# Expert weight loads of a 32-slot mixture-of-experts stage: one transfer a chunk for gate and up, expert numbers read ahead of a wait, down-projection halves reloaded one by one

## The reference, cut to what matters

```python
for e in range(N_EXPERTS):
    he = jax.nn.silu(t @ w1[e]) * (t @ w3[e])
    y = y + gates[:, e:e + 1] * (he @ w2[e]).astype(jnp.float32)
```

## Time and profile before

| what | value |
|---|---|
| median of 3 runs | 1234.81 us |
| lowest and highest | 1231.45 and 1239.08 us |
| the profiled execution's own time | 1233.89 us |
| its span, first to last instruction | 1232.0 us |
| PE busy in the span | 1091.4 us (89%) |
| DVE, ACT, POOL busy | 707.4, 514.1, 354.1 us |
| mean granted TensorE clock | 0.947 |
| chain of waits, share | PE 60%, DMA 12%, DVE 7%, issue 7% |
| of it transfers into `below` from the expert weights | 7% |
| of it SP issuing at L1370 | 3% |

### The profile page before, as it was taken

How to read it: one execution, slowest core, us unless ns; L and a number is a source line. 1 busy time by engine, 2 the same in 40 slices (tenths; PEclk the granted TensorE clock), 3 DMA queues, 4 the chain that set the end, 5 groups by cost and what they waited for, 6 DMA issues and landing times.

```text
span 1232.0 us, 18370 instructions
## 1 busy us (share of the span) xinstructions
PE 1091.4 (89%) x5873; PEld 882.0 (72%) x5873; DVE 707.4 (57%) x1348; ACT 514.1 (42%) x935; POOL 354.1 (29%) x379
## 2 busy tenths in 40 slices
PE   5999999998888899999999999974899999999930
PEld 4889899965456777777878786863777777778820
DVE  4430610136656666566566655438777777777757
ACT  4433321122531221323223233313777878778803
POOL 3100510001531111011111100101665656566657
PEclk9999999999989898898999999986999999999975
DMA  8340141141769585555655454834988786867476
GB/s 279 100 159 1 52 139 50 44 111 48 252 230 345 182 294 193 190 205 179 213 190 202 157 173 143 297 132 154 315 311 315 242 291 232 289 233 265 189 236 253
DMA packets 105765, 242.84 MB, mean 197 GB/s; under 512 B 15248, under 2 KB 63840, under 8 KB 95456
## 3 DMA queue, kind: packets, MB, share of 16 engines
q0 software_dynamic: 23328, 122.17, 28.3%
q1 hardware_dynamic: 81312, 117.42, 27.9%
q10 hardware_dynamic: 1056, 2.36, 0.6%
HBM read 243.31 MB, written 48.94 MB: 237 GB/s over the span
## 4 chain that ended last, share of the span: by engine, by line
PE 60%; DMA 12%; DVE 7%; issue 7%; POOL 5%; ACT 5%; SPq 4%; POOLq 1%; ACTq 0%; DVEq 0%
DMA below<-in_w 7%; PE ps L1027 5%; PE ps L889 4%; PE ps L907 4%; PE ps L2130 4%; PE ps L2131 4%; PE ps L2132 4%; PE ps L985 3%; PE ps L1065 3%; SPq L1370 3%; PE ps L1066 3%; PE ps L2125 3%; PE ps L2124 3%; PE ps L2126 3%; PE ps L1069 3%
## 5 line engine op out<-in xcount | busy, mean ns | idle before, releaser
L1787 DVE TENSOR_TENSOR low<-below,high 128x1024 fp32r<-128x1024 f32 x128 | 156.7, 1257 | 38.0 <-ACT high L1484 36.1
L1582 PE MATMUL ps<-high 128*128 128x512 f32 x384 | 157.1, 409 | 13.9 <-DVE low L1797 7.4
L1456 POOL TENSOR_TENSOR low<-below,high 128x1024 fp32r<-128x1024 f32 x64 | 132.8, 2076 | 97.5 <-ACT high L1504 96.4
L1583 PE MATMUL ps<-low,high 128*128 128x512 f32 x384 | 151.7, 395 | 0.0
L1584 PE MATMUL ps<-high,low 128*128 128x512 f32 x384 | 151.6, 395 | 0.0
L1484 ACT ACTIVATE high<-below 128x1024 fp32r<-128x1024 f32 x128 | 130.5, 1068 | 42.8 <-DMA below<-in_w 42.5
L626 ACT ACTIVATE arena<-ps 128x512 f32<-128x512 f32 (+8 forms) x100 | 50.0, 510 | 178.1 <-PE ps L889 177.7
L889 PE MATMUL ps<-arena 128*128 128x128 f32 (+4 forms) x613 | 96.6, 281 | 10.1 <-ACT arena L869 3.8
L770 POOL DMA_DIRECT2D high<-wo_dram x34 | 18.6, 547 | 298.9 <-PE ps L1069 287.1
L1582 PEld LDWEIGHTS ps<-high 128*128 128x128 f32 x384 | 72.9, 190 | 30.9 <-issue 15.5
L889 PEld LDWEIGHTS ps<-arena 128*128 128x128 f32 (+4 forms) x613 | 73.7, 152 | 28.6 <-issue 17.3
(11 more groups left out here) (246 smaller groups left out, 2239.2 us busy)
## 6 DMA issues: line engine op xcount, KB each, us to landing
below<-in_w SPq DMA_DIRECT2D x256, 256.0 KB
high<-wo_dram POOLq DMA_DIRECT2D x36, 1024.0 KB, 5.3
low<-wo_dram POOLq DMA_DIRECT2D x36, 1024.0 KB, 8.0
below<-in_w POOLq DMA_DIRECT2D x64, 512.0 KB
y_dram<-arena SPq DMA_DIRECT2D x32, 512.0 KB
arena<-in_x_prompt SPq DMA_DIRECT2D x15, 512.0 KB
below<-in_w_in SPq DMA_DIRECT2D x14, 512.0 KB, 7.6
out<-arena SPq DMA_DIRECT2D x9, 512.0 KB, 2.6
```

The lines of the kernel that those rows point to most:

```text
L1456: pool.tensor_tensor(w2_lo[s % UN][:, c], w2_in[:, c], w2_hi[s % UN][:, c].bitcast(F32), ALU.subtract).then_inc(s_w2lo, 1)
L1582: pe.matmul(out, x_hi, w_hi, start=start, stop=False)
L1583: pe.matmul(out, x_hi, w_lo, start=False, stop=False)
L1787: dve.tensor_tensor(chunk(w13_lo[j], c), chunk(w13_in, c), chunk(w13_hi[j], c).bitcast(F32), ALU.subtract).then_inc(s_w13lo, 1)
```

## The change

Four things are changed. (1) The host joins `w1` and `w3` along the last axis into `w13`, and SP loads a chunk of both in one transfer of 512 KB with rows of 2 KB; the waits of ACT and DVE count 16 a slot where they counted 32. (2) SP's store of output rows moves from behind the four chunks of slot s (row s - 3) to ahead of the chunks of slot s and behind the reads of the expert numbers (row s - 4); four stores are left for the end instead of three. The order of transfers on SP stays the same, but for the nine residual loads of slot 28, which now come ahead of the store of slot 25 instead of behind it. (3) POOL reads the expert numbers of slot s + 1 ahead of its waits for the high parts. (4) POOL issues the load of each half of `w2` right behind the low part of that half.

```diff
             e, new = expert(sp, s)
-            rows13 = [w[0, bass.ds(e, 1)].rearrange("e (c p) f -> p (e c) f", p=P) for w in (w1, w3)]
+            rows13 = w13[0, bass.ds(e, 1)].rearrange("e (c p) f -> p (e c) f", p=P)
+            if not isinstance(s, int) or s >= 4:
+                store_y(s - 4)
+                sp.dma_start(y_dram[bass.ds((s - 4) * P, P), :], y_row[:, j, :]).then_inc(s_yst[j], 16)
             for c in range(WC):
...
                     sp.wait_ge(s_w13lo, split)
-                for k in range(2):
-                    sp.dma_start(w13_in[:, 2 * c:2 * c + 2, k * FF:(k + 1) * FF], rows13[k][:, 2 * c:2 * c + 2, :],
-                                 cond=new).then_inc(s_w13in[c], 16)
-            if not isinstance(s, int) or s >= 3:
-                store_y(s - 3)
-                sp.dma_start(y_dram[bass.ds((s - 3) * P, P), :], y_row[:, (j + 1) % UN, :]).then_inc(
-                    s_yst[(j + 1) % UN], 16)
+                sp.dma_start(w13_in[:, 2 * c:2 * c + 2, :], rows13[:, 2 * c:2 * c + 2, :],
+                             cond=new).then_inc(s_w13in[c], 16)
...
-        for s in range(SLOT_TILES - 3, SLOT_TILES):
+        for s in range(SLOT_TILES - 4, SLOT_TILES):
...
-        def load_second(s):
-            e, new = expert(pool, s)
-            for c in range(2):
-                if s:
-                    pool.wait_ge(s_w2lo, 2 * s + c - 1)
-                pool.dma_start(w2_in[:, c], w2[0, bass.ds(e, 1), c * P:(c + 1) * P].rearrange("e p n -> p (e n)"),
-                               cond=new).then_inc(s_w2in[c], 16)
+        def load_second(s, c, e, new):
+            if s:
+                pool.wait_ge(s_w2lo, 2 * s + c - 1)
+            pool.dma_start(w2_in[:, c], w2[0, bass.ds(e, 1), c * P:(c + 1) * P].rearrange("e p n -> p (e n)"),
+                           cond=new).then_inc(s_w2in[c], 16)
...
             if s + UN < SLOT_TILES:
                 gather(s + UN)
+            if s + 1 < SLOT_TILES:
+                e, new = expert(pool, s + 1)
             for c in range(2):
                 pool.wait_ge(s_w2hi, 2 * s + c + 1)
                 pool.tensor_tensor(w2_lo[s % UN][:, c], w2_in[:, c], w2_hi[s % UN][:, c].bitcast(F32),
                                    ALU.subtract).then_inc(s_w2lo, 1)
-            if s + 1 < SLOT_TILES:
-                load_second(s + 1)
+                if s + 1 < SLOT_TILES:
+                    load_second(s + 1, c, e, new)
...
-                act.wait_ge(s_w13in[c], 32 * (s + 1))
+                act.wait_ge(s_w13in[c], 16 * (s + 1))
...
-                dve.wait_ge(s_w13in[c], 32 * (s + 1))
+                dve.wait_ge(s_w13in[c], 16 * (s + 1))
...
+    inputs["w13"] = np.concatenate([inputs["w1"], inputs["w3"]], axis=-1)
```

More of the change, by code:

```diff
@@ L104, in hybrid_layer @@
                  kv_norm, w_uq, w_uk, w_uv, hg_lb_logits, hg_gnorm, w_o, ffn_norm, w_router_group, b_router_group,
-                 w_router_expert, b_router_expert, w1, w3, w2, final_norm, table, level_masks,
+                 w_router_expert, b_router_expert, w13, w2, final_norm, table, level_masks,
                  y_prompt, y_sample, ckv_prompt, krope_prompt, hgrn_prompt, ckv_sample, krope_sample, hgrn_sample):
@@ L1447, in moe_pool @@
         gather(0)
-        load_second(0)
+        e, new = expert(pool, 0)
+        for c in range(2):
+            load_second(0, c, e, new)
         gather(1)
@@ L2216 @@
         "kv_norm", "w_uq", "w_uk", "w_uv", "hg_lb_logits", "hg_gnorm", "w_o", "ffn_norm", "w_router_group",
-        "b_router_group", "w_router_expert", "b_router_expert", "w1", "w3", "w2", "final_norm"]
+        "b_router_group", "w_router_expert", "b_router_expert", "w13", "w2", "final_norm"]
 _OUTS = [(1, 1024, D), (1, SAMPLE, D), (1, 1, 1024 + META, CR), (1, 1, 1024 + META, RD), (1, 1, HH, HK, HK),
@@ L2229 @@
     arrays, args = {}, []
+    inputs["w13"] = np.concatenate([inputs["w1"], inputs["w3"]], axis=-1)
     for name, a in [(n, np.ascontiguousarray(inputs[n])) for n in _INS] + [("table", table), ("masks", level_masks)]:
-        if name in ("w1", "w2", "w3"):
+        if name in ("w13", "w2"):
             a = np.ascontiguousarray(a.reshape(1, NG, EG, *a.shape[2:]).swapaxes(1, 2).reshape(a.shape))
```

## The result

The changed kernel takes 1237.71 us (median of 12 runs, 1234.48 to 1243.71) against 1233.45 (12 runs) of the kernel before: ratio 1.0033, 95% interval 1.0018 to 1.0048. It is slightly slower, where 1.1% faster was forecast, and stands outside the forecast's range. The profiled execution took 1234.48 us with a span of 1232.8, 0.6 us more than that of the kernel before. It was the fastest of the 12, 3.2 us under their median, so the traces show only a part of the loss of 4.3 us between the medians.

A forecast was written before the change was run, and what follows sets the result against it. PE's pace of 9.36 us a slot was the floor, expert loads adding 20.8 us. Gains of 10.5 (slots 8 to 27) and 4.0 (slots 0 to 8), less 0.5, made 14.0 us: 1221 us, range 1217 to 1223.

The forecast's parts named there:

- Halves of w2: POOL's w2 loads: half 0 reloaded 0.1 us after its low part instead of 2.1; half 1's low part 0.6 later, costing nothing.
- Slower: Rival: half 0's issue delays POOL's low part of half 1, the down product waits for it in 31 slots; 1246, chance 0.03.
- Pairs: Slots 8 to 27, a new expert every second slot: earlier last chunk removes 10.5 of 11.4 us excess, ends 4 and 11.4.
- 3.15 MB at 354 GB/s: Down weights, tokens, gate and up ahead of the last chunk's landing from about 1004: 8.9 us, landing at 1013.6 against 1016.19.
- Followers: Slots 0 to 8, new experts in succession: 4.0 of 9.4 us excess gained, ends 1.0 and 9.4.
- The engines hold the landing: Rival: the last chunk lands when the bytes are through; slots 8 to 27 give 5, slots 0 to 8 2; 1228, chance 0.27.
- One transfer a chunk: SP's chunk loads: four issues at 0.5 us each let SP follow DVE; last chunk issued 2.1 to 2.5 us earlier.
- Reads ahead of the wait: SP's expert-number reads moved ahead of the store: first chunk issued 0.9 us sooner; alone cannot be worse than nothing.
- Slot 28: Nine residual loads go ahead of slot 25's store: cost 0 with 4 us cover, 3 us once if the cover is gone.
- Rows of 2 KB: Chunk loads run at 386 GB/s instead of 354, saving 0.5 us a new expert; bounds nothing and 0.75 us.

The follow-up runs named there:

- parts 1 and 2: Kernel before with SP's side of the change only (one transfer a chunk, store behind the expert reads), POOL's code as before: 1230.84 us, ratio 0.9983.
- joined weights alone: Kernel before with only w1 and w3 joined, one 512 KB transfer a chunk in 2 KB rows: 1230.77 us, ratio 0.9961; again 1227.51, 0.9967.
- cutting w2: Kernel with SP's side of the change only, loads of w2 cut to 64 of 1024 columns from slot 1 on: 1220.34 us, ratio 0.9876.
- the order alone: Kernel before with only SP's store of output rows moved behind the expert reads and ahead of the chunks: 1236.79 us, ratio 1.0023.
- changed kernel with the cut: Changed kernel with POOL's low part of half 1 cut to 64 of 1024 columns from slot 2 on: 1225.34 us, ratio 0.9928.
- parts 3 and 4: Kernel before with POOL's side only (expert reads ahead, each w2 half loaded behind its own low part), SP as before: 1247.81 us, ratio 1.0125.
- the delay alone: Kernel before with POOL waiting for its half 0 low part and reading expert numbers between its two low parts: 1252.59 us, ratio 1.0150.
- the store behind chunk 0: Joined weights and expert reads ahead, against the kernel before, with the output rows stored after the first chunk's load: 1255.91 us, ratio 1.0192.

## Why the prediction was wrong, step by step

The forecast was 14.0 us less, and the medians show 4.3 more. Some 10 of these 18 us are the overlap, which the forecast did not have. Without it the change is worth 0.9948, some 6.4 us; the other 7.6 of the 14.0 were expected of transfers that come through more slowly than forecast. Both are estimates from ratios.

**Halves of w2** is the step that gave the wrong sign. "Cover 3.5 us, cost nothing" looked for who waits for the low part of half 1, found the down product, and stopped. The cover held. The price came from what runs beside the instruction at its new time. In the kernel before, the second of POOL's low parts starts 2.2 us after the first (896.45 and 898.64), and DVE's four hardly meet it: they take 4.82 us, and 4.63 where that low part is cut. In the changed kernel it starts 3.5 us after (997.63 and 1001.14) and meets them, which costs DVE 1.36 us more in slot 15. The delay was mis-sized too: 0.6 us forecast, 1.3 measured, since POOL's wait for its own result was not in it. The two engines shut each other out: DVE's first low part ends at 1004.36 (1004.18 + 0.18 in the chain), its own length of 1.2 us behind POOL's end at 1003.17, and not behind its own start at 1001.48. By an estimate from these rows, their need is 2 x 2.0 + 4 x 1.2 = 8.8 us of exclusive time in a slot of 9.36, so there is hardly a place to move either to. Removing the overlap turns 1.0033 into 0.9948. The rival "Slower" named this very instruction and its delay, but let it decide through the down product, and set 0.03.

The Trainium skill, SBUF — State Buffer, section Who interferes with whom, states that a DVE instruction with two SBUF inputs contends with a GpSimd instruction that reads SBUF. Section SBUF: two separate sides of that page adds that whichever of the two starts first has the shared pair of ports for its whole length, and the other "fully blocks". The traces agree in both directions (6.18 for 4.82 us on DVE, 3.04 for 2.0 on POOL). Both low parts are such instructions, and the forecast did not weigh it.

**Pairs** was mis-sized: 10.5 us forecast, 2.9 measured with parts 1 and 2, and 1.1 without the half-clock stretch. (The forecast also counted on the load of half 0 in the idle gap, which is part 4's.) The issue came earlier as said. Counted from DVE's first low part, the last chunk is issued at 5.09 us (1000.97 to 1006.06) where it was 7.43 (1001.54 to 1008.97): 2.3 of the 2.1 to 2.5. The joined weights alone do as much (1000.77 to 1005.87, 5.10), so the order adds nothing there. But ACT takes it 13.68 us after that first low part (1014.65) where it was 14.65 (1016.19): 1.0 of the 2.6. The term that failed is 3.15 MB at 354 GB/s. That rate is of chunk rows alone on the engines; the first 5 us of these bytes move at 282. Were it so for all of them, 3.15 MB would take 11.2 us and not 8.9, 2.3 more, which is an upper bound; the landing came at 1014.63 (1006.06 + 8.57), 1.0 past the forecast's 1013.6, although that execution stood 0.6 us ahead of the other at 1001.

**Followers**: 4.0 forecast, none measured. The 2 KB rows do run at 390 GB/s (396 with parts 1 and 2, 1010 to 1014), but slots 0 to 8 wait for the sum of chunks, halves and tokens, and cutting w2 shows it: 6.2 us come back there. The rival "The engines hold the landing" (1228) was nearest to parts 1 and 2, which took 1230.84; it had followers at 2 and pairs at 5, and neither came.

**One transfer a chunk** was right: SP now follows DVE, four issues in 3.65 us, and the last goes out 0.3 us after its buffer is free (1007.66 to 1007.92 in the changed kernel). Joined weights bring 0.3 to 0.4% by themselves (0.1 to 0.6% by the intervals).

**Reads ahead of the wait** "cannot be worse than nothing" was false: the order alone costs 0.2% (1.0007 to 1.0038). Counted from DVE's first low part, the first chunk goes out at 1.81 us (1001.65 to 1003.46) where it was 2.30 (1001.54 to 1003.84), 0.5 of the 0.9 forecast. The step counted SP's time alone; that a chunk that goes out sooner takes the engines from a half of w2 fits the traces and is not shown. **Slot 28** was right: ACT at L1497 waited there only for PE, and keeping the residual loads in place brought nothing.

**Rows of 2 KB**: 386 forecast, 390 and 396 measured. The Trainium skill's limit of about 358 GB/s for a core between HBM and SBUF (DMA: Bandwidth & Descriptors, section Where 436 GB/s comes from), by which longer rows bring nothing, does not hold in these traces, in which one core is at work.

## What to carry to other kernels

Before an instruction is moved, even by 1 us, lay its new place beside what the other engines run then, and ask what they share; the cover to its own consumer is only half of the question. Reckon a landing with the rate that the same mixture of transfers shows in the trace, not with the best row of the same kind, and ask whose bytes an earlier issue pushes back. Run each part of a change by itself: here only the first of four parts gained beyond the noise as it stood, and together they lost. Parts 3 and 4 were never run one by one.

## What the runs showed of the hardware

- DVE and POOL, each with a two-input `tensor_tensor` on SBUF, exclude each other: the later one waits for the earlier one's end. The mean of 128 low parts went from 1257 to 1440, 1470 and 1476 ns in the three kernels that separate POOL's two low parts, and to 1236 where one of them was cut. A DVE operation with one input in PSUM is not held: the low part of the gated rows takes 0.42 us beside POOL's low part (parts 1 and 2, 1000.02) and away from it (changed kernel with the cut, 993.61).
- Rate by row length on an engine share above 1: 354 GB/s with 1 KB, 390 and 396 with 2 KB, 405 with 4 KB. Mixed with POOL's halves and the gather: 282 to 289 at a share of 0.9.
- TensorE's granted clock fell to 0.5, 1.2 GHz, for some 3.5 us at a time, about 1.7 us lost each. From slot 0 to slot 31 the kernel before has one such stretch, at 1101, and the changed one has one at 940, so they cancel in the total. The slow kernels have more: three with parts 3 and 4 (a fourth stands 8 us ahead of slot 0), four with the delay alone, six with the store behind chunk 0; parts 1 and 2, the joined weights and the order have none in their first traces. The one at 1101:

```profile
1101.00:1105.00 4.00, 4.00 (x12) 3.10 (x11) 3.17 (x4) 4.00 (x6) 3.46 (x4) 0.57 0.50 184
```

  PE had stood idle for 0.99 and 0.61 us just before it, at 1099.45 and 1100.50, behind a slot of 11.47 us. But idle times of 0.71 and 0.61 us at 1019 brought no such stretch, and no run shows what does. If the stalls bring them, a stall is paid a second time: the five more with the store behind chunk 0 make 8.6 of its 22.6 us.
